# Differential attention as 72 equal rounds: values, sums, norm and store tile by tile

## The reference

```python
lam = jnp.exp(jnp.sum(lp[0] * lp[1])) - jnp.exp(jnp.sum(lp[2] * lp[3])) + lam_init
p1 = jax.nn.softmax(jnp.einsum("bhqd,bhkd->bhqk", q1, k1).astype(jnp.float32) * scale, axis=-1)
p2 = jax.nn.softmax(jnp.einsum("bhqd,bhkd->bhqk", q2, k2).astype(jnp.float32) * scale, axis=-1)
a = (p1 - lam * p2).astype(v.dtype)
...
o = sweep_query_blocks(block, q)          # block: a @ v for 128 queries
o = rms_norm(o, subln_w) * (1.0 - lam_init)
```

## Time and profile before

| | us |
|---|---|
| median of 3 runs | 3524.15 (3523.22 to 3524.66) |
| the profiled execution | 3526.85 |
| its span | 3525.1 |
| PE busy | 3310.3 (94%) |
| DVE, ACT, POOL busy | 1886.6, 1185.1, 945.4 |
| mean granted clock of TensorE | 0.978 of full speed |

### The profile page before, as it was taken

The page is one execution under the profiler, slowest core; times in us unless marked ns, Lnnn a source line. Parts: engine busy times, 40 slices in busy tenths (PEclk is TensorE's granted clock), DMA queues, the critical chain, the costliest instruction groups (busy, mean ns, idle before and its releaser), DMA issues. The chain is left out here.

```text
span 3525.1 us, 51658 instructions
## 1 busy us (share of the span) xinstructions
PE 3310.3 (94%) x20797; PEld 3053.4 (87%) x20797; DVE 1886.6 (54%) x2696; ACT 1185.1 (34%) x2113; POOL 945.4 (27%) x730
## 2 busy tenths in 40 slices
PE   5999999997989999999998999998898999999997
PEld 4777877776989999999988877776798999999997
DVE  4555665655165554554555566665326454555455
ACT  3344444444132212122223556665423111222122
POOL 1122221222333322233334122222143222333221
PEclk9999999998999999999999999999899999999999
DMA  6333333323211111111113111101322111111101
GB/s 243 102 99 107 103 108 99 106 80 130 84 42 42 54 42 42 36 42 36 54 30 87 40 33 28 35 24 35 111 92 65 37 42 36 42 42 53 36 30 60
DMA packets 206659, 229.78 MB, mean 65 GB/s; under 512 B 30564, under 2 KB 173533, under 8 KB 205341
## 3 DMA queue, kind: packets, MB, share of 16 engines
q1 hardware_dynamic: 186973, 162.69, 15.3%
q10 hardware_dynamic: 11664, 42.47, 3.6%
q0 software_dynamic: 7856, 22.29, 1.8%
HBM read 181.79 MB, written 31.98 MB: 61 GB/s over the span
## 5 line engine op out<-in xcount | busy, mean ns | idle before, releaser
L206 PE MATMUL psum<-Hh,wh 128*128 128x384 f32 x3360 | 1141.3, 340 | 36.8 <-ACT Hh L414 16.3
L208 PE MATMUL psum<-Hl,wh 128*128 128x384 f32 x3360 | 1129.3, 336 | 0.0
L207 PE MATMUL psum<-Hh,wl 128*128 128x384 f32 x3360 | 1128.6, 336 | 0.0
L313 DVE SCALAR_TENSOR_TENSOR x<-psum,mod,x 128x384 f32<-128x384 f32 (+2 forms) x768 | 376.8, 514 | 648.5 <-PE psum L208 603.7
L206 PEld LDWEIGHTS psum<-Hh,wh 128*128 128x128 f32 x3360 | 635.4, 189 | 48.0 <-issue 18.6
L207 PEld LDWEIGHTS psum<-Hh,wl 128*128 128x128 f32 x3360 | 635.2, 189 | 0.0
L208 PEld LDWEIGHTS psum<-Hl,wh 128*128 128x128 f32 x3360 | 634.6, 189 | 0.0
L888 POOL TENSOR_TENSOR wl<-wr,wh 128x1024 fp32r<-128x1024 f32 x88 | 219.6, 2495 | 988.2 <-ACT wh L778 988.2
L838 ACT ACTIVATE ff_u<-psum 128x768 f32<-128x768 f32 x86 | 70.0, 814 | 1092.1 <-PE psum L208 1092.1
L1050 DVE SCALAR_TENSOR_TENSOR ff_c<-ff_u,par,ff_c 128x1153 f32<-128x1153 f32 x172 | 371.5, 2160 | 15.6 <-DVE ff_c L1047 5.2
L206 PE MATMUL psum<-ff_ah,ff_dh 128*128 128x384 f32 x1056 | 364.9, 346 | 13.1 <-DVE x L313 8.3
(11 more groups left out here) (229 smaller groups left out, 4257.5 us busy)
## 6 DMA issues: line engine op xcount, KB each, us to landing
wr<-w_up SPq DMA_DIRECT2D x88, 512.0 KB, 3.8
ff_dr<-w_down SPq DMA_DIRECT2D x22, 1024.0 KB, 6.0
da_mw<-mod_w ACTq DMA_DIRECT2D x40, 512.0 KB, 3.9
wr<-mod_w ACTq DMA_DIRECT2D x40, 512.0 KB, 4.8
wr<-w_qkv_diff SPq DMA_DIRECT2D x24, 512.0 KB, 19.2
x<-x_save SPq DMA_DIRECT2D x16, 576.0 KB, 6.7
in_mw<-mod_w SPq DMA_DIRECT2D x8, 1024.0 KB, 10.6
Hh<-oh_save SPq DMA_DIRECT2D x14, 576.0 KB, 9.7
```

The lines of the kernel that those rows point to most:

```text
L206: pe.matmul(out, w_hi, m_hi, start=start, stop=False)
L207: pe.matmul(out, w_lo, m_hi, start=False, stop=False)
L208: return pe.matmul(out, w_hi, m_lo, start=False, stop=stop)
L313: last = dve.scalar_tensor_tensor(g.x[:, m, lo:hi], g.PS[:, bank, lo - n * NB:hi - n * NB], g.mod[:, gate + m, cond:cond + 1], g.x[:, m, l ...
```

## The change

The loop over heads and steps becomes one loop over 72 rounds (`ROUNDS` = 8 heads of 9 tiles, `at(r)` gives head and tile). There is no step without scores and nothing that is done only at a head's end. In round r PE makes the scores of tile r, the transposes and PV of tile r-2, ST of tile r-3 and BC of tile r-4; each for a single tile, across the border of heads. A round is written so on PE: first four blocks of T; then the wait for both exponentials of round r-1, ST, BC, the scores; then the second four blocks of T, the projection, the slice M if there is one, and PV. The ninth block of T (the "rider") goes into the free columns of W's bank.

ST, BC, ck and ko leave the two turning banks: they take columns 384 to 511 of the score banks 0, 3, 5 and 4 (`spot`). DVE does the guard sum ahead of the first maximum, the scaling between the two maxima, and the accumulation of M at the end of the round (before: at its start). The M slots of a head move from steps 1, 3, 4, 5, 7, 8 to 3 to 8, and ACT issues the next slice's loads at the round's end. The buffers `pt`, `o`, `sq`, `y`, `yh` and `yl` shrink to one tile. All heads have the same nine projections, so the one that was made ahead of head 0 (`W+`) moves into round 0. After round 71 two further rounds and four last uses empty the pipeline, with the four banks of the output projection between them. The other phases only have new arguments of shared helpers.

```diff
-        "pt": ([P, TT, 2 * P], F32), "o": ([P, 2, 2 * P], F32), "sq": ([P, 2, 2 * P], F32), "y": ([P, 2, 2 * P], F32),
+        "pt": ([P, TT, P], F32), "o": ([P, 2, P], F32), "sq": ([P, 2, P], F32), "y": ([P, 2, P], F32),
...
-    SLOTS = [(h, s) for h in range(HEADS - 1) for s in (1, 3, 4, 5, 7, 8)]
+    SLOTS = [(h, s) for h in range(HEADS - 1) for s in (3, 4, 5, 6, 7, 8)]
...
-    PROJ = [None, ("k", 1), ("k", 2), ("q", 0), ("q", 1), ("q", 2), ("v", 0), ("v", 1), ("v", 2)]
-    PV_AT, ST_AT, BC_AT = {2: [0], 4: [1], 6: [2], 8: [3], 9: [4]}, {3: [0], 5: [1], 7: [2], 9: [3, 4]}, {4: [0], 6: [1], 8: [2], 9: [3, 4]}
+    PROJ = [("k", 0), ("k", 1), ("k", 2), ("q", 0), ("q", 1), ("q", 2), ("v", 0), ("v", 1), ("v", 2)]
...
+    def weighted(r):
+        return [("PV",) + at(r - 2)] if r >= 2 else []
+    def means(r):
+        return [("ST",) + u[1:] for u in (weighted(r - 1) if r >= 1 else [])]
+    def spreads(r):
+        return [("BC",) + u[1:] for u in (weighted(r - 2) if r >= 2 else [])]
...
+    def behind(r):
+        uses, tile = [], turned_tile(r)
+        if tile and tile[1] < QT:
+            uses.append(("T",) + tile + (1,))
+            if rider(r) is None:
+                uses.append(("T",) + tile + (2,))
+        if r >= ROUNDS:
+            return uses + weighted(r)
+        h, s = at(r)
+        uses += {1: [("vt", h, 0)], 2: [("vt", h, 2)]}.get(s, [])
+        if h < LAST:
+            uses.append(project_use(r))
+        return uses + slice_uses(h, s) + weighted(r) + ([("vt", h, 1)] if s == 1 else [])
...
+            for r in range(ROUNDS):
+                for use in in_front(r):
+                    if use[0] == "T":
+                        do(use, r)
+                scores_free(r)
+                for use in in_front(r):
+                    if use[0] != "T":
+                        do(use, r)
+                scores(r)
+                for use in behind(r):
+                    do(use, r)
...
+            for r in range(ROUNDS):
+                h, s = at(r)
+                for use in means(r):
+                    mean_square(use, r)
+                maximum(r, 0)
+                for use in spreads(r):
+                    normalise(use, r)
+                maximum(r, 1)
...
+                combine(r)
+                for use in slice_uses(h, s):
+                    accumulate(use)
```

More of the change, by code:

```diff
@@ L63, in rope_tables, with __init__, bank, done @@
     return np.concatenate([cos, cos], axis=0), np.concatenate([sin, sin], axis=0)
[L66 to L111, removed]
+class Turns:
+    def __init__(self, uses, own):
+        self.order, self.place, self.prior = {}, {}, {}
+        count, turns = {}, 0
+        for use in uses:
+            assert use not in self.order
+            self.order[use] = len(self.order)
+            if use[0] in own:
+                continue
+            place, turns = "AB"[turns % 2], turns + 1
+            self.place[use], self.prior[use] = place, count.get(place, 0)
+            count[place] = count.get(place, 0) + 1
+    def bank(self, use):
+        return {"A": WORK, "B": WORK + 1}[self.place[use]]
+    def done(self, use):
+        return self.order[use] + 1
+    def wait_free(self, eng, free, use):
+        if self.prior[use]:
+            eng.wait_ge(free[self.place[use]], self.prior[use])
+    def wait_read(self, eng, free, use):
+        eng.wait_ge(free[self.place[use]], self.prior[use] + 1)
 class Chain:
@@ L1339, in phase_diff_attention @@
     Y0 = 3
[L1343 to L1364, removed]
+    def at(r):
+        return (r // TILES, r % TILES)
+    def project_use(r):
+        h, s = at(r)
+        return ("W", h + 1) + PROJ[s] if h < LAST else None
@@ L1374, in load_slice, with unit, transposed @@
         eng.dma_start(g.wr[:, 1, :, :].rearrange("p k n -> p (k n)"), rows[:, 1024:2048]).then_inc(b.mw_in, 16)
[L1376 to L1386, removed]
+    def unit(h, x):
+        return 3 * h + UNIT[x]
     def slot(h, x):
         return unit(h, x) % 2
-    def unit(h, x):
-        return 3 * h.index + UNIT[x]
+    def transposed(eng, r):
+        tile = at(r)
+        if r + 2 in RIDERS:
+            eng.wait_ge(b.turned, RIDERS.index(r + 2) + 1)
+        else:
+            eng.wait_ge(b.full, ring.done(("T",) + tile + (0 if tile[1] == QT else 2,)))
     with stack, nc.Block() as block:
@@ L1702, in scores_by_rows, with mod_piece @@
-            def scores_by_rows(h, t):
+                if tile is not None:
+                    transposes(g, pe, PS[:, bank, NB:NB + P], b.e0[:, (TILES * tile[0] + tile[1]) % 2, :], 8, 1).then_inc(b.turned, 1)
+                linear_bank(g, pe, bank, g.wh[:, slot(h, x)], g.wl[:, slot(h, x)], n).then_inc(b.full, 1)
+            def mod_piece(use):
+                m, bank = use[1], ring.bank(use)
+                ring.wait_free(pe, free, use)
+                pe.wait_ge(b.mw_in, 32 * m + 32)
+                for j in range(4):
+                    last = pe.matmul(PS[32 * j:32 * j + 32, bank, :], g.sc[:, m % KC, :], mw[j], start=True, stop=True)
+                last.then_inc(b.full, 1)
```

695 lines of the change are left out of this document (352 added, 343 removed).

## The result

| | us |
|---|---|
| median of 4 runs | 3496.86 (3493.02 to 3500.6) |
| ratio to before (3524.4, 4 runs) | 0.9921, 95% interval 0.9907 to 0.9935 |
| the profiled execution, its span | 3498.64, 3496.8 |
| PE, DVE, ACT, POOL busy | 3309.4, 1876.2, 1196.5, 1011.3 |
| mean granted clock of TensorE | 0.979 |

27.5 us less, faster by 0.8%; 3490 was predicted. The page's line of busy times shows how little the totals say: PE's work is the same to 1 us, although it has 576 instructions more.

What follows compares the result with a forecast made beforehand. PE, busy for 94% of the span, was taken to bound the kernel. Gains of 14 (heads 1 to 6), 6 (head 0), 9 (head 7) and 5 (tail) sum to 34 us: 3493 profiled, median 3490, range 3475 to 3506.

Steps and rivals of the forecast that it cites:

- heads 1 to 6: PE work and waits sum to 97.9 us a head instead of 100.2, giving back 14 us.
- `da_acc`: Next round's first T waits for DVE's accumulation of M: 1.8 us in round 7, 0.55 and 0.4 elsewhere, 2.75 a head.
- The rounds with MT: With MT, PV and the next T wait for its bias: 0.65 us a head on average; MT's work 0.3.
- small waits of the sum: Waits in a head: ST 1.35 us, switches 1.8, value transposes 1.1, ck and ko 0.3, unknown small ones 0.75.
- PV at 0.112: PV by tile takes 0.112 us per 128-column instruction: +0.15 us a pair, +0.6 a head.
- the rival on weight loads: Weight loads set PV's pace at 0.190 us an instruction: 78 us more, 3568; chance 0.04.
- Head 0: Rounds 0 and 1 have no T or PV yet; exponentials set their pace: 92.5 us, 6 less.
- the tail: After the last scores, each output-projection bank covers a chain: 26.7 us against 31.7, 5 less.
- Head 7: Without projections the scores-maxima-exponentials chain sets the pace: 7.3 us a tile, 58.4 in all, 9 less than 67.5.
- The clock: Rival: up to 15 new pauses in head 7 and rounds 7 lower PE's clock, 3.4 us each: 3541, slower; chance 0.09.
- The rival that the waits don't bite: Accumulation comes in time and small waits are shadows: 4.2 us a head, 29 more gained, 3461; chance 0.18.
- That heads get nothing: Rival: another 0.3 us waited each round on an ACT copy or bank, 2.5 a head: 3507; chance 0.15.

Runs made afterwards that it cites:

- experiment 2: Changed kernel with slices M in rounds 2, 3, 4, 5, 6, 8 of a head instead of 3 to 8: 3484.08 us.
- experiment 5: Kernel before the change with only PV of a pair made as two passes of 128 columns, tile by tile: 3524.73 us, ratio 1.0004.
- experiment 6: Changed kernel with POOL's two output-weight splits in head 7 cut to one column, leaving the low parts out: 3493.36 us.
- experiment 7: Changed kernel with the accumulation of M ahead of `combine` on DVE and slices M in rounds 2, 3, 4, 5, 6, 8: 3481.51 us.
- experiment 8: Experiment 7's kernel with ACT's square and copy of the prompt tile's result between the two exponentials in head 7's second round: 3485.58 us.
- experiment 9: Experiment 8's kernel with the low parts of head 7's output weights made by DVE behind the second maximum instead of by POOL: 3479.47 us.
- experiment 3: Changed kernel with a fourth operation of the query rotation on DVE in round 7 instead of round 8: 3512.72 us.
- experiment 4: Changed kernel with the ninth block of T in a turn of its own in the two banks, not in W's bank: 3528.47 us.

## Why the prediction held, and where it did not

**The sum was right for heads 1 to 6, with errors that cancel.** 97.9 was said, 97.2 measured. Round 7 was said to wait 1.8 and waits 1.25: DVE's chain was counted as 9.55 and takes 9.4, PE's as 7.95 and takes 8.2, and the 0.2 added for an instruction held by POOL didn't occur there. Rounds 4 and 5, for which 0.55 and 0.4 were taken, don't wait. Round 4 has one rotation less, 9.4 - 1.25 = 8.15 for DVE, which is just what PE needs.

So `da_acc` costs 1.25 in a head that has it, not 2.75. The rounds with MT were under-estimated instead, at 0.65 a head and 0.3 of work: the one that falls into round 7 of head 2 takes 3.4 more than the other rounds 7, part of it by the clock, three others take 1.57, 1.58 and 0.89 more than 11.09, and the one in round 7 of head 6, where no slice is left, takes 11.91, 2.0 more than a round 7 without a slice (9.88 in experiment 2). Together that is 9.5, or 1.6 a head. A slice itself was counted as 0.99 and costs 1.21. These make some 1.9 us a head more than was counted. `da_acc` gives 1.7 of them back (1.25 in five of six heads), and small waits of the sum another 0.9; which of them was not worked out. That the total came out within 0.7 is luck in part. The late load costs 0.56 once and a low stretch 1.54 once (the round 8 of 11.32), 0.35 a head against 0.3.

**PV at 0.112 was right** (experiment 5), and the rival on weight loads is out: at 0.190 that experiment would have cost (0.190 - 0.112) x 18 = 1.4 us a tile in 64 tiles, 90 us; its median is 0.5 us above that of the kernel before.

**Head 0** was said to take 92.5 and takes 93.3; **the tail** 26.7 and 27.1. Each bank of the output projection covers a chain, as said: the first begins at 861.92, the last at 876.14, and PE pauses in between nowhere for more than a few tenths. But the tail before, against which the gain is reckoned, ran its first 9 us at half clock (a low stretch of 10.2 us from 876.8 on); PE's timeline there has the PV of two tiles at 6.05 instead of 4.05:

```profile
883.19 6.05 PE L1687 MATMUL psum<-da_pt,da_v 128*128 128x256 f32 x18 [0.67 <-ACT da_pt L1486]
```

So about 2 of the 4.7 us gained are the clock, and not banks that cover a chain; the prediction has no such term. In the same way the clock of head 7 rose from 0.79 to 0.92; how much of its 2.9 us that makes was not separated.

**Head 7 is the term that was mis-sized:** 58.4 was said, 64.6 measured; of the 9 us only 2.9 came. The price of an undisturbed tile was good, 7.16 against 7.3. Set against 7.16 a round, the excess of 64.57 - 8 x 7.16 = 7.3 us is: 1.0 + 1.3 in the two rounds behind a POOL split; 2.2 in the sixth, all of it the low clock (its PV alone takes 1.9 more), gone with the split in experiment 6, and absent also from some kernels that have the split; 2.2 in the third, of which 1.4 is the scores at half speed (3.2 us instead of 1.8) and 0.7 the value transposes, whose copy stands ahead of the first exponential on ACT; 0.55 in the second, for value transposes too. The prediction had the held instruction in its rows and used it in round 7, where it does not occur in the changed kernel, and not in head 7, where it does; and it counted the value transposes in heads with projections only. (In experiments 7 to 9 the held instruction does occur in rounds 7 of heads 0 to 3, 2.34 to 2.37 us long, and those rounds still take 9.9: they have no slice whose accumulation could come late.)

That DVE's instruction is held by POOL's is shown by experiments 6 and 9: it takes 0.15 as soon as POOL's is short or gone, with nothing else changed on DVE in experiment 6. Experiment 8 shows it inside one kernel: its first split (801.62, 2.37 us) falls between two of these small instructions, and the fourth distance is 7.16 although the split was made; its second meets one, and the fifth distance is 8.47. In the changed kernel the instruction ends when POOL's operation ends (813.79 + 2.33 and 813.64 + 2.48, both 816.12). The Trainium skill's page "SBUF — State Buffer", section "Who interferes with whom", states that a DVE instruction with two inputs in SBUF contends with a GpSimd instruction that reads SBUF, that such contention is an exclusive lock, and that the order of issue decides who blocks. The trace agrees: L1845 has two such inputs, POOL's split began 0.15 us before it, and it was held to the split's end. In the kernel before the record of the held instruction begins 0.01 us ahead of POOL's (501.38 and 501.39), so the order can't be read from starts there.

**The clock** was a rival at 0.09, with up to 15 new low stretches and an end on the slower side. It didn't come about: between the first scores and the end of the tail four low stretches begin (two in heads 1 to 6, of 3.4 each, and two in head 7, of 3.4 and 6.8) beside the rest of one that began at 110.9, where before there were seven. The low stretches in the middle of the kernel that were named as a sign of being wrong did come, twice (387.4 and 489.8). And it was near. The waits for `da_acc` stopped at 1.4 us; with 2.15 in experiment 3 six low stretches came. Of the rule of the Trainium skill's page "TensorE: Matmul & The Clock Gate", section "A second HAM failure mode: psum-queue depth-cycling", that short idles between groups of matmuls bring the clock down again and again, the runs here show both sides: one low stretch behind five pauses of 1.4 us, five behind five of 2.15.

**The rival that the waits don't bite** (3461) was right on rounds 4 and 5 and wrong on round 7. **That heads get nothing** was wrong, but experiment 4 shows how near it was: a copy waited for once in a round is all it takes.

**Open:** why the pause in the second round of head 7 is followed by 3.4 us at the low clock in the changed kernel (pause of 3.15), 6.8 in experiment 7 (3.14), 13.7 in experiment 8 (1.68) and 6.8 in experiment 9 (1.68). The third round of head 7 was not cured. That the copies in the two turning banks are gone is told by the waits and by experiment 4; what each other part of the change is worth (ST and BC in the score banks, uses spread over the border of heads) was not tried by itself.

## What to carry to other kernels

When a loop is evened out into equal rounds, put the operation that frees a bank for the bottleneck engine ahead of the operations that nobody waits for until a round later: here one swap of two DVE statements was worth another 12.7 us by the medians (10.6 in heads 1 to 6 of the profiles), nearly half of the whole change. Give a small piece of work the free columns of a bank that is in turn anyway before giving it a turn of its own; that was worth 31.6. And look where the filler of the long rounds is missing (here the last head): there a side operation on POOL that shares time with a tiny DVE instruction goes straight onto the path.

## What was not expected of the hardware

A one-element DVE instruction of 0.15 us took 2.33 us beside a POOL operation of 2.48. No other small DVE instruction of the attention phase took over 1 us in the changed kernel but these two; in the kernel before there are five, of 2.39 to 2.41, each beside a split of 2.36 or 2.37. The same subtraction of 1024 columns takes 2.35 to 2.77 us on POOL in the heads and 1.22 on DVE. And 0.75 us more in five pauses (1.4 to 2.15) was followed by five low stretches instead of one.
